# Two mixing attentions regrouped into turns of two units, and the router's last logits moved ahead of table and key products

## The chip, the cores and the metric

The kernel runs on one core of one Trainium2 chip. The metric is the device time in microseconds (us), lower being better; the median of three runs is compared. Engine names are those of the profile: PE (TensorE matmuls), PEld (its weight loads), DVE (VectorE), ACT (ScalarE), POOL (GpSimd), SP (SyncE, which issues most DMAs). All data are float32.

## What is computed

The reference is a two-block transformer on 512 tokens of width 1024; each block has two layers. The first block's layers end with a mixture of experts. For every token a router picks a group and two experts:

```python
g_logits = xt @ w_group
_, g_sel = lax.top_k(g_logits + b_group, 1)
e_logits = (xt @ w_expert).reshape(T, N_GROUPS, EXPERTS_PER_GROUP)[tok, g_sel]
_, e_local = lax.top_k(e_logits + e_bias, TOP_K)
```

The second block's two layers begin with a mixing attention each. Layer 0 is the dilated attention (16 heads of 64, three dilation patterns, which the kernel folds into one additive mask), layer 1 the differential attention (8 pairs of heads):

```python
p = softmax(q k^T / 8 + mask);           o = p v                       # dilated, per head
p = softmax over keys, for two maps;     o = (p[0] - lam * p[1]) v      # differential, per pair
o = rms_norm(o, sub_g) * (1 - lam_init)                                # differential only
```

Both are followed by the output projection `o @ w_out`, a cross attention to 256 memory tokens and a gated feed-forward layer.

## The kernel before

All five engines run one program each, in an order written out by hand; they meet on semaphores. `ps` is PSUM in eight banks of 512 columns, `TT` = 4 tiles of 128 tokens, `KC` = 8 chunks of 128 channels.

**Units.** An attention is cut into `UNITS` = 32 units: unit `n` is chunk `c = n // 4` (two heads, or one pair) and query tile `t = n % 4`. `PAIRED` = 16. For each chunk, q and k are first transposed (`turn_q`, `turn_k`, bank 7) and copied out (`queries` on ACT, `keys` on DVE).

**Dilated** (lines 2036 to 2186). PE: `scores(n)` (L2059), two products of 64 rows by 512 columns that lie in the two row halves of the array, into banks `2 * (n % 2)` and the next; it waits for `masked(n - 2)`. DVE: `masked(n)` (L2118) adds the mask, writes the tile and its row maximum. ACT: `expo(n)` (L2155), exponent and row sum. DVE: `invert(n)` (L2125). POOL: scales by the reciprocal (L2184). PE: `turn_probs(n)` (L2070), eight transposes into banks 4 and 5. ACT and DVE: `copy_probs(n)` (L2163, L2131). PE: `output(b, part)` (L2083), the product with v of two units at once into column halves of the array, in two parts of eight instructions. ACT: `finish(c)` (L2167) copies the finished chunk. The PE order is per unit `i`: `scores(i)`, `turn_probs(i - 2)`, a turn of q or k in two units of four, `output(i // 2 - 2, i % 2)`. The output projection starts after `finish(7)` (L2769).

**Differential** (lines 2213 to 2430). PE: `scores(n)` (L2247), as above, waiting for `expo(n - 2)`. DVE: `maximum(n)` (L2310). ACT: `expo(n)` (L2357). DVE: `invert(n)` (L2317). POOL: `weigh(n)`, which is a 128x1 product (L2400), a drain, and the scaling of the second map (L2402). DVE: `mixed(n)` (L2323), first map times reciprocal plus the weighed second map; both are in SBUF. PE: `turn_diff(n)` (L2256), four transposes. ACT: `copy_diff(n)` (L2365). PE: `output(n)` (L2265). DVE: `finish(n)` (L2329) copies the output, ACT: `square(n)` (L2374). Per chunk, POOL's `roots(c)` (L2408 on) and `scale_out(c)` (L2417) normalize, PE turns the result (`turn_out`, L2236) and ACT copies it (`copy_out`, L2379). In DVE's order, `invert(i - 1)` and `mixed(i - 2)` follow `maximum(i)`. In POOL's order `roots(c)` follows `weigh(4c + 11)` and `scale_out(c)` follows `weigh(4c + 12)`. Once the last scores are done, `out_products` of chunks 0 to 3 (L2742) are put between the remaining steps.

**Router** (`first_out`, lines 1102 to 1197; `router`, lines 1615 on). After the mixer's output projection, token tile 3 is transposed (`turn_raw`, L1233), its logits are computed (`route_tile`, L431), DVE chooses the experts (`choose`), PE counts the ranks (`count_before` L1452, `count_inside` L1459), DVE marks the slots (`place`), PE sums the marks into a table (`table_tile`, L1497), and POOL's first `gather_rows` (L1738) fetches rows by that table. The rows are transposed at L1748. Between these steps stand products for the memory keys (`key_products`, L1339; ACT reads them at L1348), which are needed in any case. POOL issues the store of `normed` (L1249), and every gather waits for it.

```python
key_products(name, key_q, 0, keys, range(2))
turn_raw(name, eng, y0, TT - 1)
share_tile(name, eng, j0, TT - 1, buf)
place_tile(name, eng, l, TT - 2)
key_products(name, key_q, 0, keys, range(2, 4))
table_begin(name, eng, l)
route_tile(name, eng, l, j0, TT - 1)
```

Of the kernel before, what the change touches and what calls it, by code (L numbers as in the profile page):

```python
# [8 lines left out]
TT = S // P  # L9
KC = D // P  # L10
# [69 lines left out]
def program(nc, a):  # L80
# [5 lines left out]
    with ctx:  # L86
# [1015 lines left out]
        def first_out(name, eng, l, m_norm):  # L1102
# [92 lines left out]
            key_products(name, key_q, 0, keys, range(2, 4))  # L1195
            table_begin(name, eng, l)
# [408 lines left out]
        def table_begin(name, eng, l):  # L1605

            if name == "pe":
                open_bank(eng, until=(table_ready, l + 1))
                at["table"] = count[("pe", "bank")] - 1
                for t in range(TT - 2):  # L1610
                    table_tile(eng, l, t, bank_of(at["table"]))
            else:
                at["table"] = take(name, "bank")

        def router(name, eng, l):

            w = first_keys_w(name)
            table_q = at["table"]
            if name == "pe":
                open_bank(eng, "dve")  # L1620
                count_q = count[("pe", "bank")] - 1
                count_before(eng, l, TT - 1, bank_of(count_q))
                table_tile(eng, l, TT - 2, bank_of(table_q))
            else:
                count_q = take(name, "bank")
            key_products(name, at["first_keys"], 0, w, range(4, KC))
            key_read(name, eng, l, 0, 0, at["first_keys"], counted=False)
            key_q = key_open(name, 0)
# [5 lines left out]
            key_products(name, key_q, 1, w, range(2))  # L1634
# [16 lines left out]
            key_products(name, key_q, 1, w, range(2, KC))  # L1651
# [384 lines left out]
        def dilated_pe(pe):  # L2036
# [36 lines left out]
            def output(b, part):  # L2073
                c, half = divmod(b, 2)
                if part == 0:
                    pe.wait_ge(l_probT_act, 2 * b + 2)
                    pe.wait_ge(l_probT_dve, 2 * b + 2)
                    if half == 0 and c:
                        pe.wait_ge(l_out_read, c)
                for s in range(2 * part, 2 * part + 2):  # L2080
# [4 lines left out]
                if part:  # L2085
                    m.then_inc(l_out, 1)
# [3 lines left out]
            for i in range(UNITS + 3):  # L2090
                if i < UNITS:
                    scores(i)
                if 0 <= i - 2 < UNITS:
                    turn_probs(i - 2)
                if i % TT == 1 and i // TT + 1 < KC:
                    turn_q(i // TT + 1)
                if i % TT == 2 and i // TT + 1 < KC:
                    turn_k(i // TT + 1)
                if i >= 4:
                    output(i // 2 - 2, i % 2)  # L2100
            output(PAIRED - 1, 1)

        def dilated_dve(dve):
# [30 lines left out]
            for i in range(UNITS + 2):  # L2134
                if i < UNITS:
                    masked(i)
                if 0 <= i - 1 < UNITS:
                    invert(i - 1)
                if i % TT == 2 and i // TT + 1 < KC:
                    keys(i // TT + 1)  # L2140
                if 0 <= i - 2 < UNITS:
                    copy_probs(i - 2)

        def dilated_act(act):
# [25 lines left out]
            for i in range(UNITS + 3):  # L2170
                if 0 <= i - 2 < UNITS:
                    copy_probs(i - 2)
                if i < UNITS:
                    expo(i)
                if i % TT == 1 and i // TT + 1 < KC:
                    queries(i // TT + 1)
                if i >= 6 and i % TT == 2:
                    finish(i // TT - 1)
# [34 lines left out]
        def differential_pe(pe, l):  # L2213
# [57 lines left out]
            for i in range(UNITS + 5):  # L2271
                if i < UNITS:
                    scores(i)
                if 0 <= i - 5 < UNITS:
                    output(i - 5)
# [1511 lines left out]
```

## Time and profile before

| what | value |
|---|---|
| median of 3 runs | 2943.52 us (2942.08 to 2946.53) |
| the profiled execution | 2939.72 us |
| its span, first to last instruction | 2937.9 us |
| PE busy | 2819.7 us, 96% of the span |
| DVE, ACT, POOL busy | 38%, 23%, 17% |
| mean granted PE clock | 0.993 of full speed |
| dilated attention | 1333.6 to 1450.1 us |
| differential attention, to the end of its first output products | 2214.9 to about 2346 us |
| the router, layer 0 and layer 1 | 306 to 324 us and 887 to 904 us |

All stage positions are microseconds from the start of the span. A timeline row gives start, duration, engine, line, operation, tiles, and how many instructions are merged in it; in brackets stands the engine's idle time before it and what ended that. One fp32 matmul of the source appears as two PE instructions. A windows row gives, for a stretch, the busy time and instructions of each engine, the granted PE clock and the DMA share.

### The profile page before, as it was taken

The numbers are of one execution on the slowest core, as the hardware profiler recorded it, in microseconds if no ns is written. First come the engines' busy times: TensorE is split into PE (matmuls) and PEld (weight loads), VectorE is DVE, ScalarE is ACT, GpSimd is POOL, SyncE is SP. The second block draws the span as 40 slices with busy tenths as digits, with TensorE's granted clock in tenths as the row PEclk, the third lists the DMA queues.
The fourth block names the chain that finished last, engine by engine and source line by source line (L and its number), as shares of the span: only waits on it lengthen the run. The fifth ranks groups of instructions, "written<-read, shape, count | busy, mean of one in ns | idle before, by whom it ended". The sixth has DMA issues, their size and how long they took to land.

```text
span 2937.9 us, 32164 instructions
## 1 busy us (share of the span) xinstructions
PE 2819.7 (96%) x12444; PEld 1898.3 (65%) x12444; DVE 1111.5 (38%) x2252; ACT 662.8 (23%) x1512; POOL 511.3 (17%) x785
## 2 busy tenths in 40 slices
PE   8999999799999987999999999999999999999998
PEld 4565543255655432685566688888686575788887
DVE  4543311154433111445432333354446432333354
ACT  3333110133331101105422211101206512211100
POOL 3101111131111111113200022201114410122201
PEclk9999999999999999999999999999999999999999
DMA  3206799821158998320021222222220121222222
GB/s 134 75 29 251 295 425 424 367 110 56 46 241 330 424 424 358 143 86 30 29 79 37 79 91 89 72 79 94 86 87 29 34 82 33 82 87 86 72 87 86
DMA packets 106579, 422.13 MB, mean 144 GB/s; under 512 B 10096, under 2 KB 14320, under 8 KB 91440
## 3 DMA queue, kind: packets, MB, share of 16 engines
q1 hardware_dynamic: 93104, 387.01, 33.9%
q0 software_dynamic: 12736, 30.84, 2.8%
q8 instruction: 104, 1.70, 0.2%
q10 hardware_dynamic: 576, 2.10, 0.2%
q14 instruction: 59, 0.48, 0.0%
HBM read 408.63 MB, written 27.26 MB: 148 GB/s over the span
## 4 chain that ended last, share of the span: by engine, by line
PE 77%; issue 9%; DMA 7%; DVE 2%; ACT 2%; POOL 1%; POOLq 1%; DVEq 0%; SPq 0%; ACTq 0%
PE ps L2536 35%; DMA ring_feat<-in_w 6%; PE ps L1773 6%; PE ps L2769 5%; PE ps L431 5%; PE ps L1112 3%; PE ps L2742 3%; PE ps L1814 3%; PE ps L2643 2%; PE ps L2789 2%; PE ps L3103 2%; PE ps L1339 2%; PE ps L2247 1%; PE ps L2265 1%; PE ps L2083 1%
## 5 line engine op out<-in xcount | busy, mean ns | idle before, releaser
L431 PE MATMUL ps<-ring_feat 128*128 128x512 f32 (+2 forms) x704 | 275.4, 546 | 4.9 <-DMA ring_feat<-in_w_lat 2.8
L2536 PE MATMUL ps<-ring_feat 128*128 128x256 f32 x1216 | 276.9, 379 | 0.8 <-ACT big L287 0.8
L2536 PE MATMUL ps<-big 128*128 128x256 f32 x1200 | 268.1, 379 | 0.0
L2536 PEld LDWEIGHTS ps<-ring_feat 128*128 128x128 f32 x1216 | 231.2, 190 | 33.1 <-issue 2.1
L2536 PEld LDWEIGHTS ps<-big 128*128 128x128 f32 x1200 | 228.3, 190 | 30.7
L431 PEld LDWEIGHTS ps<-ring_feat 128*128 128x128 f32 x704 | 133.0, 192 | 130.8 <-issue 93.8
L2769 PE MATMUL ps<-ring_feat 128*128 128x512 f32 x320 | 139.4, 593 | 0.7 <-ACT ring_feat L2167 0.7
L2536 PE MATMUL ps<-tmp 128*128 128x256 f32 x576 | 128.2, 379 | 0.0
L2536 PE MATMUL ps<-ring_feat,tmp 128*128 128x256 f32 x544 | 126.6, 379 | 0.0
L2536 PEld LDWEIGHTS ps<-tmp 128*128 128x128 f32 x576 | 109.6, 190 | 14.8
L1112 PE MATMUL ps<-ring_feat 128*128 128x512 f32 x256 | 114.7, 600 | 0.0
L2536 PEld LDWEIGHTS ps<-ring_feat,tmp 128*128 128x128 f32 x544 | 103.4, 190 | 14.0
L1789 DVE TENSOR_TENSOR tmp<-tmp,ps 128x256 f32<-128x256 f32 x32 | 13.5, 422 | 250.0 <-ACT tmp L1783 250.0
L2769 PEld LDWEIGHTS ps<-ring_feat 128*128 128x128 f32 x320 | 60.1, 190 | 73.3 <-issue 72.2
L1828 POOL DMA_INDIRECT expert_out<-tmp,route_i x32 | 32.1, 1004 | 405.1 <-ACT tmp L1823 393.6
L1773 PE MATMUL ps<-big,tmp 128*64 128x512 f32 x416 | 93.4, 596 | 6.2 <-DVE tmp L1757 4.7
L2536 PE MATMUL ps<-ring_feat,big 128*128 128x256 f32 x400 | 95.5, 379 | 0.0
L2725 DVE TENSOR_TENSOR big<-ps,par 128x512 f32<-128x512 f32 x32 | 22.1, 692 | 189.6 <-ACT big L2721 189.6
L1773 PE MATMUL ps<-ring_feat,tmp 128*64 128x512 f32 x384 | 86.2, 596 | 5.3 <-DMA ring_feat<-in_w 2.9
L1757 DVE TENSOR_TENSOR tmp<-ps,par 128x512 f32<-128x512 f32 x64 | 41.2, 686 | 131.1 <-PE ps L1748 131.1
L2742 PE MATMUL ps<-ring_feat 128*128 128x512 f32 x192 | 85.7, 596 | 5.0 <-ACT ring_feat L3002 2.7
L2536 PEld LDWEIGHTS ps<-ring_feat,big 128*128 128x128 f32 x400 | 76.1, 190 | 10.3
(497 smaller groups left out, 4630.8 us busy)
## 6 DMA issues: line engine op xcount, KB each, us to landing
big<-in_w SPq DMA_DIRECT2D x36, 2048.0 KB, 22.6
ring_feat<-in_w SPq DMA_DIRECT2D x36, 2048.0 KB, 29.2
ring_feat<-in_w_gate_up SPq DMA_DIRECT2D x22, 2048.0 KB, 8.0
ring_feat<-in_w_mix_in SPq DMA_DIRECT2D x12, 2048.0 KB, 8.2
e_spare<-in_w SPq DMA_DIRECT2D x12, 1792.0 KB, 25.7
par<-in_w SPq DMA_DIRECT2D x12, 1536.0 KB, 23.7
ring_feat<-in_w_down SPq DMA_DIRECT2D x12, 1536.0 KB, 6.7
tmp<-in_w_mem_kv SPq DMA_DIRECT2D x6, 2048.0 KB, 25.3
```

The lines of the kernel that those rows point to most:

```text
L431: yield T.matmul(bank, lhs(k), rhs(k), start=k == 0, stop=k == n - 1)
L1112: m = T.matmul(bank, featv[:, k, t * P:(t + 1) * P], w[:, k, :], start=k == 6, stop=k == 2)
L1339: m = T.matmul(bank_of(q)[:, 0:N_MEM], w[:, k, i * P:(i + 1) * P], memT[:, k, :], start=k == 0, stop=k == KC - 1)
L1757: m = V.tensor_tensor(e_xT[p % 2][:, 4 * b:4 * b + 4, :], ps[:, b, :].rearrange("p (k s) -> p k s", k=4), g[:, 4 * b:4 * b + 4].unsqueeze( ...
L1773: m = T.matmul(ps[h, u, :], e_xT[s][:, k, h], e_half(l, c, i)[k % 4], start=k == 0, stop=k == KC - 1)
L1814: m = T.matmul(ps[h, 6 + half, :], e_hT[:, k, h], e_half(l, c, i)[2 * k + half], start=k == 0, stop=k == 1)
L2536: m = T.matmul(to, lhs[:, j, :], rhs[:, j, :], start=start and j == 0, stop=stop and j == chunks - 1)
L2643: yield T.matmul(bank, featv[:, k, t * P:(t + 1) * P], w[:, k, :], start=k == 0, stop=k == KC - 1)
L2742: m = T.matmul(begun["banks"][t], featv[:, k, t * P:(t + 1) * P], begun["w"][:, k, :], start=k == 0, stop=k == KC - 1)
L2769: yield T.matmul(bank, featv[:, k, t * P:(t + 1) * P], w[:, k, :], start=k == 0, stop=k == KC - 1)
L2789: m = T.matmul(bank[:, tokens], w[:, k, (f % 4) * P:(f % 4 + 1) * P], featv[:, k, tokens], start=k == 0, stop=k == KC - 1)
L3103: m = T.matmul(bank[:, tokens], w[:, kk, o:o + P], featv[:, kk, tokens], start=kk == 0, stop=kk == KC - 1)
```

## The change

Nothing is computed differently; the orders are new. In both attentions PE issues the scores of two units back to back. In the dilated attention the two parts of `output` are joined, and at the end output-projection products stand between the last steps. In the differential attention DVE, ACT and POOL get new orders too. In the router, `route_tile` of the last tile comes before the table and before two key products, and the key products stand elsewhere in the chain.

```diff
 # first_out
             place_tile(name, eng, l, TT - 2)
-            key_products(name, key_q, 0, keys, range(2, 4))
-            table_begin(name, eng, l)
             route_tile(name, eng, l, j0, TT - 1)
 # router (table_begin is gone)
+                open_bank(eng, until=(table_ready, l + 1))
...
                 count_before(eng, l, TT - 1, bank_of(count_q))
-                table_tile(eng, l, TT - 2, bank_of(table_q))
+                for t in range(TT - 1):
+                    table_tile(eng, l, t, bank_of(table_q))
-            key_products(name, at["first_keys"], 0, w, range(4, KC))
+            key_products(name, first_q, 0, w, range(2, 4))
 # count_inside, place
-            key_products(name, key_q, 1, w, range(2))
+            key_products(name, first_q, 0, w, range(4, 6))
 # last table_tile, table_ready
-            key_products(name, key_q, 1, w, range(2, KC))
+            key_products(name, first_q, 0, w, range(6, KC))
+            key_read(name, eng, l, 0, 0, first_q, counted=False)
+            key_q = key_open(name, 0)
+            key_products(name, key_q, 1, w, range(KC))
 # dilated_pe
+            for p in range(PAIRED):
+                scores(2 * p)
+                scores(2 * p + 1)
+                if p >= 1:
+                    turn_probs(2 * p - 2)
+                if p % 2 == 0 and p // 2 + 1 < KC:
+                    turn_q(p // 2 + 1)
+                if p % 2 == 1 and p // 2 + 1 < KC:
+                    turn_k(p // 2 + 1)
+                if p >= 2:
+                    output(p - 2)
+                if p >= 1:
+                    turn_probs(2 * p - 1)
+            turn_probs(UNITS - 2)
+            output(PAIRED - 2)
+            turn_probs(UNITS - 1)
+            pe.wait_ge(l_masked, UNITS)
+            out_begin(pe)
+            pe.wait_ge(l_out_read, KC - 2)
+            out_products(pe, 0, range(KC - 2))
+            output(PAIRED - 1)
+            for t in range(1, TT):
+                if t == 1:
+                    pe.wait_ge(l_out_read, KC - 1)
+                out_products(pe, t, range(KC - 1))
 # dilated_dve, per p: masked(2p), masked(2p+1), copy_probs(2p-2), invert(2p), keys if p is odd, invert(2p+1), copy_probs(2p-1)
 # dilated_act, per p: expo(2p), copy_probs(2p-2), queries if p is even, expo(2p+1), finish(p//2-1) if p is odd, copy_probs(2p-1)
 # differential_pe
+            for p in range(PAIRED):
+                m, odd = divmod(p, 2)
+                scores(2 * p)
+                scores(2 * p + 1)
+                if not odd and m >= 4:
+                    turn_out(m - 4)
+                if p >= 2:
+                    output(2 * p - 4)
+                if p >= 1:
+                    turn_diff(2 * p - 2)
+                if odd and m + 1 < KC:
+                    turn_k(m + 1)
+                if p >= 2:
+                    output(2 * p - 3)
+                if not odd and m + 1 < KC:
+                    turn_q(m + 1)
+                if p >= 1:
+                    turn_diff(2 * p - 1)
...
 # differential_dve
+            for p in range(PAIRED):
+                maximum(2 * p)
+                if p >= 1:
+                    mixed(2 * p - 1)
+                maximum(2 * p + 1)
+                if p >= 2:
+                    finish(2 * p - 4)
+                invert(2 * p)
+                if p % 2 == 1 and p // 2 + 1 < KC:
+                    keys(p // 2 + 1)
+                if p >= 2:
+                    finish(2 * p - 3)
+                mixed(2 * p)
+                invert(2 * p + 1)
...
 # differential_act, per p: expo(2p), copy_out if even and late, copy_diff(2p-2), expo(2p+1), square(2p-4), queries if even, copy_diff(2p-1), square(2p-3)
 # differential_pool
-                if n >= 11 and n % TT == 3:
-                    roots((n - 11) // TT)
-                if n >= 12 and n % TT == 0:
-                    scale_out((n - 12) // TT)
+                if n >= 8 and n % TT == 0:
+                    roots((n - 8) // TT)
+                if n >= 9 and n % TT == 1:
+                    scale_out((n - 9) // TT)
```

## Rows read from the trace of the kernel before

**Rows 1.** Page, part 1: busy time of the engines over the span.

```profile
PE 2819.7 (96%) x12444; PEld 1898.3 (65%) x12444; DVE 1111.5 (38%) x2252; ACT 662.8 (23%) x1512; POOL 511.3 (17%) x785
```

**Rows 2.** Windows: dilated start and middle, differential middle (PE, PEld, DVE, ACT, POOL, PEclk, DMA).

```profile
1333.00:1347.00 14.00, 9.58 (x46) 5.03 (x47) 7.42 (x22) 7.29 (x16) 3.00 (x5) 0.88 0.43 150
1399.00:1412.00 13.00, 12.83 (x90) 7.17 (x86) 8.34 (x25) 8.38 (x23) 4.97 (x8) 1.00 0.00 0
2256.00:2270.00 14.00, 14.00 (x93) 9.38 (x91) 10.65 (x19) 12.23 (x38) 10.23 (x21) 1.00 0.01 2
```

**Rows 3.** Timeline of the dilated attention, PE: scores, transposes, output.

```profile
1381.50 1.13 PE L2059 MATMUL ps<-tmp 64*128 64x512 f32 x4
...
1385.03 1.13 PE L2059 MATMUL ps<-tmp 64*128 64x512 f32 x4
...
1386.09 1.09 PE L2070 MATMUL ps<-cst,tmp 128*128 128x128 f32 x8
...
1387.11 1.08 PE L2083 MATMUL ps<-tmp,big 128*64 128x256 f32 x8
...
1388.13 1.13 PE L2059 MATMUL ps<-tmp 64*128 64x512 f32 x4
...
1425.45 1.13 PE L2059 MATMUL ps<-tmp 64*128 64x512 f32 x4
```

**Rows 4.** Timeline of the dilated attention's end and the projection behind it, PE.

```profile
1442.45 1.06 PE L2070 MATMUL ps<-cst,tmp 128*128 128x128 f32 x8 [1.23 <-ACT tmp L2163]
...
1446.47 2.89 PE L2083 MATMUL ps<-tmp,big 128*64 128x256 f32 x24
...
1450.05 12.28 PE L2769 MATMUL ps<-ring_feat 128*128 128x512 f32 x28 [0.69 <-ACT ring_feat L2167]
```

**Rows 5.** Timeline of the differential attention, PE: scores, output, transposes; the fifth is twelve units on.

```profile
2239.34 1.13 PE L2247 MATMUL ps<-tmp 64*128 64x512 f32 x4
...
2240.40 1.16 PE L2265 MATMUL ps<-big,tmp 128*128 128x128 f32 x8
...
2241.39 0.60 PE L2256 MATMUL ps<-cst,tmp 128*128 128x128 f32 x4
...
2241.92 1.13 PE L2247 MATMUL ps<-tmp 64*128 64x512 f32 x4
...
2276.43 1.13 PE L2247 MATMUL ps<-tmp 64*128 64x512 f32 x4
```

**Rows 6.** Timeline of the differential attention, DVE and POOL.

```profile
2222.70 0.15 DVE L2317 RECIPROCAL stat<-stat 128x2 f32<-128x2 f32 x1
...
2223.36 0.69 POOL L2402 TENSOR_SCALAR tmp<-tmp,stat 128x512 f32<-128x512 f32 x1 [0.17 <-issue]
...
2226.18 0.73 DVE L2323 SCALAR_TENSOR_TENSOR tmp<-tmp,stat 128x512 f32<-128x512 f32 x1
...
2226.83 1.22 DVE L2310 TENSOR_REDUCE stat<-ps 128x2 f32<-128x1024 f32 x1
...
2242.26 0.96 POOL L2402 TENSOR_SCALAR tmp<-tmp,stat 128x512 f32<-128x512 f32 x1 [0.17 <-issue]
...
2265.72 0.24 POOL L2408 TENSOR_SCALAR stat<-stat 128x4 f32<-128x4 f32 x1
...
2267.82 0.33 POOL L2400 TENSOR_TENSOR stat<-stat 128x1 f32<-128x1 f32 x1
```

**Rows 7.** Timeline of the router, PE, layer 0; the last row is layer 1's.

```profile
309.24 1.98 PE L431 MATMUL ps<-par,ring_feat 128*128 128x36 f32 x16
...
312.29 3.52 PE L1339 MATMUL ps<-cst,ring_feat 128*128 128x256 f32 x8
...
323.34 1.09 PE L1748 MATMUL ps<-cst,tmp 128*128 128x128 f32 x8 [0.52 <-DMA tmp<-normed,route_i]
...
893.23 2.00 PE L1339 MATMUL ps<-cst,ring_feat 128*128 128x256 f32 x8
```

**Rows 8.** Window of one microsecond in layer 0's router (columns as in Rows 2).

```profile
312.00:313.00 1.00, 1.00 (x10) 0.87 (x9) 0.77 (x6) 0.00 (x0) 0.00 (x0) 0.50 0.88 352
```

More of the change, by code:

```diff
@@ L1603, in gate_weights, with router @@
                             gate.unsqueeze(1).to_broadcast([P, 2, TT]), ALU.mult)
-        def table_begin(name, eng, l):
+        def router(name, eng, l):
+            w = first_keys_w(name)
+            first_q = at["first_keys"]
             if name == "pe":
                 open_bank(eng, until=(table_ready, l + 1))
[L1609 to L1619, printed above, removed]
+                table_q = count[("pe", "bank")] - 1
                 open_bank(eng, "dve")
@@ L2071, in turn_probs, with output @@
                 m.then_inc(l_probs_turned, 1)
-            def output(b, part):
+            def output(b):
                 c, half = divmod(b, 2)
[L2075 to L2080, printed above, removed]
+                pe.wait_ge(l_probT_act, 2 * b + 2)
+                pe.wait_ge(l_probT_dve, 2 * b + 2)
+                if half == 0 and c:
+                    pe.wait_ge(l_out_read, c)
+                for s in range(TT):
                     for j in range(2):
@@ L2084, in output @@
                                      l_probT[b % 2][:, j, s, :], start=s == 0, stop=s == TT - 1)
-                if part:
-                    m.then_inc(l_out, 1)
+                m.then_inc(l_out, 1)
             turn_q(0)
             turn_k(0)
[L2090 to L2101, printed above, removed]
+            for p in range(PAIRED):
[23 more added lines that the diff above has]
+                out_products(pe, t, range(KC - 1))
         def dilated_dve(dve):
@@ L2133, in dilated_dve @@
             keys(0)
[L2134 to L2142, printed above, removed]
+            for p in range(PAIRED):
+                masked(2 * p)
+                masked(2 * p + 1)
+                if p >= 1:
+                    copy_probs(2 * p - 2)
+                invert(2 * p)
[3 more added lines that the diff above has]
+                if p >= 1:
+                    copy_probs(2 * p - 1)
+            copy_probs(UNITS - 2)
+            copy_probs(UNITS - 1)
         def dilated_act(act):
@@ L2169, in dilated_act @@
             queries(0)
[L2170 to L2178, printed above, removed]
+            for p in range(PAIRED):
+                expo(2 * p)
+                if p >= 1:
+                    copy_probs(2 * p - 2)
+                if p % 2 == 0 and p // 2 + 1 < KC:
+                    queries(p // 2 + 1)
+                expo(2 * p + 1)
+                if p >= 3 and p % 2 == 1:
+                    finish(p // 2 - 1)
+                if p >= 1:
+                    copy_probs(2 * p - 1)
+            copy_probs(UNITS - 2)
+            copy_probs(UNITS - 1)
+            finish(KC - 1)
         def dilated_pool(pool):
```

99 lines of the change are left out of this document (52 added, 47 removed).

## The prediction

> **What bounds the kernel now.** I first read the page's busy times: PE is busy in 96% of the span, no other engine in half of it [rows 1]. So a gain must take time out of PE's own sequence, and it can be lost only where another engine makes PE wait. The windows show the same inside both attentions: 12.83 of 13 us and 14.00 of 14 us of PE busy [rows 2]. But the reader should not stop there. In the differential stage DVE, ACT and POOL are busy for 10.65, 12.23 and 10.23 us of the 14 [rows 2]; all four engines are near their limit, and the order in which they hand work on counts. In the dilated stage DVE and ACT use 8.3 of 13 us and POOL 5.0, which leaves room.
>
> Then the timeline, since a busy PE need not be working at its pace. In the dilated stage scores start at 1385.03, transposes at 1386.09, the output part at 1387.11, the next scores at 1388.13: 1.06, 1.02 and 1.02 us, a unit of 3.10 us [rows 3]. What does each group need by itself? A pass of 512 columns takes 12.28/28 = 0.44 us in the projection, start of the next pass 0.43 [rows 4]; a unit's scores are two passes in each row half side by side, 0.86. In the undivided run of 24 output instructions, 16 more than usual took 2.89 - 1.08 = 1.81 us, 0.90 per eight with a short wait in it, so 0.86 as well [rows 3, 4]. I take 0.86 for all three groups. What is left, 0.20 behind scores and 0.16 behind each of the others, comes wherever the shape that PE uses changes (64 rows, full, 64 columns), and three times per unit. It is not the semaphore: the second part of an output has no wait of its own, and its gap is the same. These gaps are what the change goes after. The Trainium skill says so too (TensorEngine Tiling (Array Packing), Key Properties): changing the tiling mode drains the engine. It gives no price.
>
> **Dilated attention, steady part.** A unit with a turn of q or k takes 1385.03 - 1381.50 = 3.53, so a turn costs 0.43. A chunk of four units takes (1425.45 - 1385.03)/3 = 13.47 us [rows 3]. That is 4 x 3.10 + 2 x 0.43 = 13.26 and 0.21 of waiting behind ACT's `finish`. After the change a pair is two scores 1.72 + 0.20, transposes 0.86, a turn 0.43, a gap 0.16, output 1.72 + 0.16, transposes 0.86 + 0.16: 6.27 us, and a chunk 12.54. It saves 0.93. Can the others follow? 13 us of the stage hold 13/3.37 = 3.9 units, in which DVE is busy for 8.34, ACT for 8.38 and POOL for 4.97 us [rows 2]: 4.3, 4.3 and 2.6 us for two units, all under 6.27. In latency, the transposes of unit i stand two units and the next scores behind its own scores, 2 x 3.10 + 1.06 = 7.3 us where no turn lies between, and PE doesn't wait for POOL there today [rows 3]. In the new order they stand a pair and two scores behind, 6.27 + 1.92 = 8.2 us. So I see no new wait, and the 0.21 goes, since `finish` now stands behind the exponents. Seven and a half chunks: -7.0 us.
>
> **Dilated start and drain.** The start is a chain with nothing in flight, and PE's granted clock is 0.88 there [rows 2]. Two scores go first as before, but the second transposes now stand behind `turn_k` and wait for two copies: +0.6. The drain of before runs from the last scores, 1425.45 + 12.61 (three more plain units and the wait) = 1438.1, to the projection at 1450.05: 12.0 us for nine groups of 0.86, so 4.3 lost; one wait of 1.23 is in the rows [rows 4]. Afterwards six products of 0.86 cover the copy ahead of the last output, and seven per tile cover the last `finish`; what stays is a wait of about 1.3 for a copy ahead of `turn_probs(30)` and some gaps: -2.2. The projection does not get longer, since these are its own products done earlier. **Dilated: -8.6**, bounds -5 (half of the gaps stay) and -11 (no loss at the start, the wait of 1.3 gone).
>
> **Differential attention.** Here scores to output take 1.06, output to transposes 0.99, transposes to scores 0.53: 2.58 per unit; twelve units took 2276.43 - 2241.92 = 34.51 us, 11.50 per chunk with two to three turns [rows 5]. By PE alone a pair would need 1.92 + 0.99 + 0.43 + 0.89 + 0.53 = 4.76 and a chunk 9.52 + 1.1 = 10.6. But PE does not decide alone. DVE's new order puts `mixed(2p - 1)` ahead of `maximum(2p + 1)` and `invert(2p + 1)` behind `mixed(2p)`. `mixed` waits for POOL's `weigh`, and `weigh` waits for `invert`. So the two engines hand each unit to and fro with nothing overlapped: invert(2p), weigh, mixed(2p), invert(2p + 1), weigh, mixed(2p + 1), maximum(2p + 3), finish, invert(2p + 2). In the old order `mixed` came one turn later, and the loop reached over two units. The durations: reciprocal start to the end of `weigh` 2224.05 - 2222.70 = 1.35 when nothing disturbs POOL, mixed 0.65 to the next instruction, the reduction 1.15 (busy for 1.22, but the next begins before its end), `finish` about 0.2 (an estimate, for 128 columns where the reduction has 1024) [rows 6]. A pair takes 2 x 1.35 + 2 x 0.65 + 1.15 + 0.2 = 5.35; a chunk 10.7. `roots` (2.10 us from 2265.72 to 2267.82) now stands between two `weigh` calls, where only mixed and the next invert, 0.9, run beside it: +1.2. And it overlaps with `mixed`, both of whose inputs are in SBUF. L2402 takes 0.96 instead of 0.69 in such a place [rows 6], so I add 0.3: 12.2 us per chunk from the third chunk on, 0.7 more than now.
>
> The Trainium skill bears on this (SBUF - State Buffer, Who interferes with whom): a DVE instruction with two SBUF inputs keeps GpSimd's reads off the port they share. The two durations of L2402 agree. It helps here as well, since `weigh` no longer runs beside `mixed`.
>
> Sum: six chunks x 0.7 = +4.2; the second chunk, before any `roots`, -1.0; the start, where a longer chain must pass before the pairs flow, +1.0; the drain, whose steps are covered by output products before and after, -1.2. That is +3.0; I take **+2.5**, since some of `roots` may hide while a turn of q, k and output makes PE late. Bounds: -5 (PE alone: 11.50 - 10.6 = 0.9 on six chunks) and +10 (each `weigh` 0.27 longer, 1.1 per chunk more).
>
> **Router.** Both layers. The logits move ahead of four key instructions, 1.1 us at the pace of the eight that take 2.00 [rows 7], and of the first tables, but must then wait some 0.4 (an estimate) for the transposed tile's copy. In the chain from the logits to the table stood twelve key instructions, eight of them 3.52 us in layer 0 [rows 7]; now eight short ones stand there. I estimate that the table is ready 2.5 us sooner. Against it: every gather also waits for the store of `normed`, which is not moved, and PE waits only 0.52 us for the gathered rows today [rows 7]. The key products are done in any case. So at most 0.5 per layer, less the new short waits: -0.3. Against it stands the clock. In layer 0 the granted clock is at half, 1.2 GHz instead of 2.4 [rows 8], right after the logits, and eight key instructions take 3.52 us where layer 1 has 2.00 [rows 7]. In the new order transposes, logits, counts and tables follow each other with no key product between; a fall of the clock in layer 1 too costs about 1.5. No row shows the new order, so I take the two together as 0, bounds -1 and +4.
>
> **Sum.** -8.6 + 2.5 + 0 = -6.1 us. The profiled execution took 2939.72, 3.8 below the median of 2943.52; against its own time 2933.6, against the median 2937.4. No DMA is moved past another on POOL's or SP's queue; the load of the memory keys for the cross attention waits for the last output and so starts ahead of most of the projection, as it does now.
>
> **Rivals.** (A) *The differential loop does not bind*, because PE's turns are late enough to cover POOL. Then that stage gives -5, the whole -13.5: 2930. For it: DVE is idle for a part of each turn. Against it: the loop is a chain by program order, and it adds up to more than PE's 10.6. (B) *`weigh` stays at its contended length or the loop is longer still*: differential +10, the whole +1: 2945, no change. For it: most of the 32 calls took 0.96; against it, they ran beside `mixed`, and in the new order they cannot. (C) *The gaps do not belong to the change of shape* but to each group, so that pairs save nothing. Only drain and `finish` are left, -4, with the differential loop unchanged: -1.5, 2942. The undivided 24 instructions speak against it [rows 4]. (D) *PE falls to half clock in the differential stage.* New waits of about 1.5 us per chunk leave PE less busy. One stretch at half clock cost 3.52 - 2.00 = 1.5 us in the router [rows 7, 8]. In the steady part of both attentions the clock is at full today [rows 2]. If it fell in each of seven chunks for two such stretches, that is 7 x 3.0 = 21 us, the whole +15, 2958; it decides from 12 us on, which is eight stretches, where the sum passes +5.9.
>
> **How the numbers follow.** A measurement of this kernel can tell 0.2%, 5.9 us. Forecast (differential between 0 and +5, total -3 to -10): 0.62, half of it beyond 5.9. A: 0.17, all faster. B: 0.10, nearly all unchanged. C: 0.06, unchanged. D: 0.05, slower. Faster 0.31 + 0.17 and a little from the dilated bound, 0.50; slower 0.05 and a part of B, 0.07; the rest, 0.43, within. The range from 2930 to 2945 takes in the forecast, most of A and half of B.
>
> **What would show it.** Dilated: scores starts in pairs 0.86 apart, pairs 6.27 apart, a chunk 12.5 against 13.47; the projection's first products between the last output steps. If pairs are 6.7 apart, the gap theory is wrong. Differential: chunks of 12.2, PE waiting for L2304 or L2323, POOL's L2402 at 0.69, and DVE waiting for L2402. Chunks of 10.6 mean A, of 13 and more B. Router: L1641 some 2.5 us nearer to the logits, the gather where it was in layer 1, and the granted clock at half behind the logits in one or both layers. The forecast is wrong if any stage outside these three moves by over 2 us.

## The result, and the profile after it

The changed kernel took 2944.88 us, median of 12 runs (2942.93 to 2952.22); the kernel before, timed beside it, 2940.30 (2937.08 to 2946.53, 12 runs). The ratio is 1.0016, 95% interval 1.0009 to 1.0024: 4.7 us slower (2.6 to 7.1), where 6.1 us faster was forecast. The profiled execution has a span of 2941.9 us against 2937.9, also +4.0. The difference is within the bound of 5.9 us, so by that bound it is no change; but it is of the other sign, and it hides three parts that are each as large as itself or larger.

PE's busy time fell by 2.8 us [rows 1] and the span grew by 4.0, so PE waits longer. Page, part 1, of the changed kernel:

```profile
PE 2816.9 (96%) x12444; PEld 1904.2 (65%) x12444; DVE 1111.0 (38%) x2252; ACT 662.7 (23%) x1512; POOL 509.1 (17%) x785
```

The windows of the same stretches as in [rows 2], the first moved by the 6 us that the dilated stage now starts later (columns: length, PE, PEld, DVE, ACT, POOL, PEclk, DMA share, GB/s):

```profile
1339.00:1353.00 14.00, 10.20 (x40) 5.06 (x40) 7.36 (x24) 7.10 (x16) 3.37 (x5) 0.76 0.42 150
1399.00:1412.00 13.00, 13.00 (x92) 7.99 (x90) 8.83 (x27) 8.92 (x22) 5.87 (x10) 1.00 0.01 1
2256.00:2270.00 14.00, 12.20 (x73) 8.07 (x72) 9.20 (x17) 9.88 (x31) 8.60 (x17) 0.88 0.01 2
```

The middle of the dilated stage is better filled than before. In the differential stage PE is busy for 12.20 us of 14 instead of 14.00, every engine does less, and the granted clock averages 0.88.

**Where the time went.** I compared the starts of the same work in both timelines. The transposes of the first gathered rows are at 326.21 instead of 323.34 [rows 7], 2.9 us late; in layer 1 they are 6.7 us late. The dilated stage starts 6.3 late, and the memory queries behind its output projection start 1.8 early: the stage gave 8.1. Up to the differential stage 1.0 of it is lost again (PE waits 0.78 us for a copy ahead of the second part of these queries), and the differential stage then costs 4.8. 6.3 - 8.1 + 1.0 + 4.8 = 4.0, the difference of the spans.

*Dilated*, PE's timeline, one pair and its ends, against [rows 3, 4]:

```profile
1404.51 1.99 PE L2051 MATMUL ps<-tmp 64*128 64x512 f32 x8
1406.43 1.09 PE L2062 MATMUL ps<-cst,tmp 128*128 128x128 f32 x8
1407.35 0.60 PE L2034 MATMUL ps<-cst,big 128*128 128x128 f32 x4
1407.88 1.95 PE L2074 MATMUL ps<-tmp,big 128*64 128x256 f32 x16
1409.76 1.09 PE L2062 MATMUL ps<-cst,tmp 128*128 128x128 f32 x8
1410.79 1.99 PE L2051 MATMUL ps<-tmp 64*128 64x512 f32 x8
...
1446.26 5.32 PE L2784 MATMUL ps<-ring_feat 128*128 128x512 f32 x12
1451.51 1.95 PE L2074 MATMUL ps<-tmp,big 128*64 128x256 f32 x16
```

A pair takes 1410.79 - 1404.51 = 6.28 us (forecast 6.27), with no wait in it, and twelve products stand ahead of the last output.

*Differential*, the vector engine and POOL around one pair with `roots`, against [rows 6]:

```profile
2256.82 0.75 DVE L2347 SCALAR_TENSOR_TENSOR tmp<-tmp,stat 128x512 f32<-128x512 f32 x1 [0.98 <-POOL tmp L2445]
...
2257.56 1.20 DVE L2334 TENSOR_REDUCE stat<-ps 128x2 f32<-128x1024 f32 x1
2260.62 0.75 DVE L2347 SCALAR_TENSOR_TENSOR tmp<-tmp,stat 128x512 f32<-128x512 f32 x1 [1.85 <-POOL tmp L2445]
2261.29 1.22 DVE L2334 TENSOR_REDUCE stat<-ps 128x2 f32<-128x1024 f32 x1
...
2256.87 0.80 POOL L2451 TENSOR_SCALAR stat<-stat 128x4 f32<-128x4 f32 x1
...
2258.51 1.04 POOL L313 TENSOR_TENSOR stat<-stat 128x4 f32<-128x4 f32 x1
2259.52 0.19 POOL L2443 TENSOR_TENSOR stat<-stat 128x1 f32<-128x1 f32 x1
2259.89 0.69 POOL L2445 TENSOR_SCALAR tmp<-tmp,stat 128x512 f32<-128x512 f32 x1 [0.17 <-issue]
2260.78 2.20 POOL L2460 TENSOR_SCALAR big<-big,stat 128x128 f32<-128x128 f32 x4 [0.19 <-issue]
```

The four instructions of `roots` (L2451 to L313) keep POOL from 2256.87 to 2259.52, 2.65 us. The second weighing of the pair (L2443, L2445) stands behind them, the mixing (L2347) waits 1.85 us for it, and the next maximum (L2334) stands behind the mixing. L2451 takes 0.80 beside a mixing, where the same instruction took 0.24 [rows 6]. `scale_out` (L2460) follows behind the second weighing. PE's first scores of a chunk and their wait for the key copy, which is queued behind all this:

```profile
2250.89 1.99 PE L2259 MATMUL ps<-tmp 64*128 64x512 f32 x8 [1.33 <-DVE tmp L2328]
...
2263.41 3.39 PE L2259 MATMUL ps<-tmp 64*128 64x512 f32 x8 [1.33 <-DVE tmp L2328]
```

From the third on chunks take 12.47, 12.53, 13.26, 12.52 and 12.24 us (11.5 before, the mean of three [rows 5]). After one of the waits the scores take 3.39 instead of 1.99: half clock, once behind the start of the stage, in the chunk of 13.26.

*Router*, layer 0, against [rows 7]; first SyncE's and POOL's queues in the kernel before (the last line is the store's time to its landing):

```profile
311.24 0.33 SPq L1707 DMA_DIRECT2D ring_feat<-in_w  x1
...
309.75 0.62 POOL L1249 DMA_DIRECT2D normed<-tmp  x1 [1.47 <-ACT tmp L333]
319.02 1.12 POOL L1738 DMA_INDIRECT tmp<-normed,route_i  x1 [8.65 <-DVEq L1644]
...
normed<-tmp POOLq DMA_DIRECT2D x1, 512.0 KB, 5.5
```

and in the changed kernel:

```profile
310.02 0.33 SPq L1699 DMA_DIRECT2D ring_feat<-in_w  x1
...
309.73 0.62 POOL L1247 DMA_DIRECT2D normed<-tmp  x1 [1.47 <-ACT tmp L333]
321.82 1.12 POOL L1730 DMA_INDIRECT tmp<-normed,route_i  x1 [11.48 <-DMA normed<-tmp]
...
normed<-tmp POOLq DMA_DIRECT2D x1, 512.0 KB, 11.2
```

Then PE in the changed kernel:

```profile
311.43 2.07 PE L1337 MATMUL ps<-cst,ring_feat 128*128 128x256 f32 x4
...
326.21 1.09 PE L1740 MATMUL ps<-cst,tmp 128*128 128x128 f32 x8 [1.77 <-DMA tmp<-normed,route_i]
```

What the two queues moved in 312 to 314 us, the kernel before first and then the changed one, and in 314 to 320 us of the changed one (q1 is SyncE's queue, q0 is POOL's):

```profile
q0 software_dynamic: 131, 0.48, 60.2%
q1 hardware_dynamic: 30, 0.31, 38.1%
...
q1 hardware_dynamic: 39, 0.44, 69.9%
q0 software_dynamic: 42, 0.17, 21.7%
...
q1 hardware_dynamic: 112, 1.64, 68.8%
q0 software_dynamic: 96, 0.34, 13.9%
```

Two things are new. SyncE's 2 MB load of slot FEAT waits for the last logits and so is issued 1.2 us sooner, 0.3 us behind the start of the store of `normed` instead of 1.5. The store lands 11.2 us after its issue, in layer 1 11.3, where it took 5.5 and 7.3 before. In the kernel before, 131 packets of its queue run within 2 us, against 30 of SyncE's. In the changed kernel POOL's queue has 144 packets and 0.52 MB, the store's, spread from 311 to 321 us. They run beside those of the load, also 144 (288 and 4.19 MB for two loads), about one for one. The gather, which waited for the table in layer 0 before (DVEq), now waits for the store. The second new thing is the clock, which is at half in both layers for some 7 us (four key products take 2.07 instead of 1.1):

```profile
312.00:318.00 6.00, 6.00 (x24) 4.58 (x23) 1.91 (x10) 0.00 (x0) 0.00 (x0) 0.50 0.93 345
896.00:902.00 6.00, 6.00 (x23) 4.59 (x23) 1.90 (x10) 0.00 (x0) 0.00 (x0) 0.51 0.97 374
```

### The profile page after: what moved, and what is told of

The parts are those of the page before. It is cut to its first block, busy times and chain, and to the rows that moved or that the text cites. A ratio compares the mean times of both kernels' runs of the same rounds, so it can differ in the third digit from the quotient of the medians.

```text
span 2941.9 us, 32161 instructions
## 1 busy us (share of the span) xinstructions
PE 2816.9 (96%) x12444; PEld 1904.2 (65%) x12444; DVE 1111.0 (38%) x2252; ACT 662.7 (23%) x1512; POOL 509.1 (17%) x785
## 4 chain that ended last, share of the span: by engine, by line
PE 72%; issue 11%; DMA 8%; POOL 3%; DVE 2%; ACT 2%; POOLq 1%; DVEq 0%; SPq 0%; ACTq 0%
PE ps L2578 35%; DMA ring_feat<-in_w 6%; PE ps L1765 6%; PE ps L431 4%; PE ps L2784 4%; PE ps L2811 4%; PE ps L1806 3%; PE ps L1112 2%; PE ps L2685 2%; PE ps L2831 2%; PE ps L3145 2%; PE ps L1337 1%; PE ps L2062 1%; PE ps L2074 1%; PE ps L2051 1%
## 5 line engine op out<-in xcount | busy, mean ns | idle before, releaser
L2578 PEld LDWEIGHTS ps<-ring_feat 128*128 128x128 f32 x1216 | 230.9, 190 | 34.5 <-issue 3.3
L431 PEld LDWEIGHTS ps<-ring_feat 128*128 128x128 f32 x704 | 132.7, 191 | 131.0 <-issue 93.6
L2784 PEld LDWEIGHTS ps<-ring_feat 128*128 128x128 f32 x256 | 47.6, 190 | 64.4 <-issue 57.5
L2811 PEld LDWEIGHTS ps<-ring_feat 128*128 128x128 f32 x256 | 48.0, 190 | 57.4 <-issue 57.4
```

The source lines that it names most:

```text
L431: yield T.matmul(bank, lhs(k), rhs(k), start=k == 0, stop=k == n - 1)
L2578: m = T.matmul(to, lhs[:, j, :], rhs[:, j, :], start=start and j == 0, stop=stop and j == chunks - 1)
L2784: m = T.matmul(begun["banks"][t], featv[:, k, t * P:(t + 1) * P], begun["w"][:, k, :], start=k == 0, stop=k == KC - 1)
L2811: yield T.matmul(bank, featv[:, k, t * P:(t + 1) * P], w[:, k, :], start=k == 0, stop=k == KC - 1)
```

## The experiments

Each ratio is to the kernel before, timed on the same chip; the groups of runs were on four chips, so runs of two groups are compared by their ratios. The profiled executions differ by up to 4.3 us ahead of any edit (first key products of layer 0 at 304.2 to 308.5), so inside the router I read a distance: from the first key products of the last tile (305.09 before) to the transposes of the first gathered rows (323.34), 18.25 us in layer 0 and 16.60 in layer 1.

**Each part alone.** First the router's part.

> Only the router's part of the change; both attentions stay as before. Theory (late gather): the changed kernel's gather starts 2.8 us later in layer 0 and 6.9 in layer 1 than before, the second less the first being 4.0 of its own, and nothing behind the router gives it back before the dilated stage. So the whole is +6 to +7 us against the kernel before, and the first pass of the dilated scores starts 6.3 us later. Rival (the router is worth 0, as predicted, and the shift seen behind it comes from something in the changed attentions, such as another placing of the code): within 1 us of the kernel before.

Ratio 1.0021 (1.0012 to 1.0030): +6.2 us. Distances 20.48 and 19.85 us; POOL waits 10.9 and 11.1 us behind the store for it to land. The loss is the router's own.

The dilated part:

> Only the dilated part. Theory (the pairs save the gaps between shapes, as in the changed kernel's trace): chunks of 12.5 us, the stage 8.1 us shorter, of which 0.8 to 1.0 is lost again at the start of the memory queries behind it; the whole -7 to -8 against the kernel before. Rival (the gaps do not belong to the shapes): chunks of 13.4, the whole -2 to -3.

Ratio 0.9973 (0.9963 to 0.9982): -7.9 us. Four pairs take 1381.76 - 1356.65 = 25.11 us, a chunk 12.56. The gaps do belong to the changes of shape:

```profile
1369.20 1.99 PE L2059 MATMUL ps<-tmp 64*128 64x512 f32 x8
1371.12 1.09 PE L2070 MATMUL ps<-cst,tmp 128*128 128x128 f32 x8
...
1375.48 1.99 PE L2059 MATMUL ps<-tmp 64*128 64x512 f32 x8
```

The differential part:

> Only the differential part. Theory (the loop DVE, PE, ACT, DVE, POOL, DVE binds, longer than predicted): chunks of 12.2 to 12.6 us against 11.2 to 11.65, the stage +4.8, the whole +4.8 against the kernel before, between +4 and +6. Rival (the stage was long because its start was shifted by what stands ahead of it, so that the roots met other work): +2.5 or less.

Ratio 1.0019 (1.0009 to 1.0028): +5.6 us, chunks of 12.5 to 13.3 from the third on, the half clock in the same chunk (scores of 3.58 us). The three parts sum to 6.2 - 7.9 + 5.6 = +3.9; the whole change gave +4.7 (2.6 to 7.1).

**The router's load.** With the store first, that is, with SyncE's load waiting until the store has landed:

```
                 sp.wait_ge(bank_full, feat_free[l])
+                sp.wait_ge(normed_rest, 16 * (TT - 1) * (l + 1))
                 load_chunk(sp, l, FEAT)
```

> The router's part alone, and SyncE issues the 2 MB weight load of slot FEAT only once the store of the normed rows has landed. Theory DMA order (the store, issued in the same microsecond as before, lands 11.2 us after its issue instead of 5.5 because the 2 MB load was issued ahead of it): the store lands after some 5 us again in both layers, the gather starts about 1 to 2.5 us sooner than in the kernel before, as the table is ready sooner, and the whole is -2 to +3 us against the kernel before; what is left above that is the half clock, about 1.5 us for each stretch. Rival (clock alone): the gather is late because the products behind the logits run at half clock and delay the table; then this wait brings nothing, the gather of layer 1 starts over 5 us later than before and the whole stays at +6.

Ratio 1.0020 (1.0011 to 1.0029): +5.9, outside what my theory expected and the rival's total. But the gather of layer 1 starts only 0.3 us later than before, counted from the first key products, not over 5, so it is not the rival's mechanism either. The order did what it should to the store: it lands after 5.7 us in layer 0 and 6.0 in layer 1, and the gather of layer 0 starts 1.7 us nearer to the first key products than before. But the distances are 19.37 and 19.23. In layer 0 the load, now at 315.13, is in flight when the gather is issued, and the rows come 7.1 us behind the gather, before 4.3:

```profile
317.02 1.12 POOL L1730 DMA_INDIRECT tmp<-normed,route_i  x1 [7.00 <-DVEq L1633]
...
324.11 1.09 PE L1740 MATMUL ps<-cst,tmp 128*128 128x128 f32 x8 [1.56 <-DMA tmp<-normed,route_i]
```

So in layer 0 I had only moved the collision from the store to the gather. In layer 1 PE does not wait for the rows at all: it is late itself, at half clock. To take the load away from both:

```
+                for s in range(2):
+                    sp.wait_ge(rows_in[s], 16 * (PAIRS // 2 * l + 1))
                 load_chunk(sp, l, FEAT)
```

> The changed router alone, and SyncE issues the 2 MB load of slot FEAT behind the landing of the first two gathers (its first reader comes 30 us later). Theory (the 2 MB load, wherever it starts, delays the small transfer issued just behind it: the store in the change, the gather in the two runs with the store first): the store lands after 5 to 6 us, the gather after 4, and what is left is PE's own time at half clock: 19 us from the first key products to the transposed rows at most in both layers, with no wait for the gathered rows over 0.5; the whole +1.5 to +4 against the kernel before. Rival (the clock costs nothing where the gather is waited for, so that the transfers are all of the router's loss): 17 to 18 us in both layers, the whole -1 to +1.

Ratio 0.9998 (0.9989 to 1.0007). Distances 16.59 and 19.17: the same code twice in one execution, once at full clock and once at half (the two ends of each distance, then a window of 7 us in each layer, PEclk behind the POOL column):

```profile
305.31 1.03 PE L1337 MATMUL ps<-cst,ring_feat 128*128 128x256 f32 x4
...
321.90 1.03 PE L1740 MATMUL ps<-cst,tmp 128*128 128x128 f32 x8
...
886.65 1.03 PE L1337 MATMUL ps<-cst,ring_feat 128*128 128x256 f32 x4
...
905.82 1.03 PE L1740 MATMUL ps<-cst,tmp 128*128 128x128 f32 x8
...
311.00:318.00 7.00, 6.73 (x58) 5.40 (x57) 4.71 (x26) 0.38 (x1) 1.18 (x2) 1.00 0.36 145
892.00:899.00 7.00, 7.00 (x49) 5.58 (x49) 3.10 (x19) 0.29 (x1) 0.00 (x0) 0.56 0.44 178
```

In neither layer do the rows make PE wait. Seven microseconds at half clock cost 2.6 us once the transfers are out of the way. The total is below what was expected, +1.5 to +4, and inside the rival's -1 to +1; in the profiled execution that is because layer 0 had full clock, and how the other executions ran is not known.

**The key products.** With the store first, key products 2 and 3 again ahead of the last logits:

> As the run with the store first, but key products 2 and 3 (four instructions of 256 columns, 1.11 us) stand ahead of the last logits again, as before the change; the rest of the new router order stays. Theory clock (the run of narrow instructions from the last transposes over logits, counts and tables to the next key products is what PE's clock falls after): that run is broken by 1.1 us of wide products, the half clock goes from 7 us in each layer back to 3.4 us or none, and the stretch from the first key products to the first transposes of the gathered rows takes 17 to 18 us in both layers instead of 19.4 and 19.2; the whole is 2 to 4 us below the run with the store first, -2 to +1 against the kernel before. Rival (those stretches are long because the products that are now behind the logits have nothing to hide the gather's own latency): still over 19 us in both layers, the whole as with the store first.

Ratio 1.0011 (1.0002 to 1.0020): +3.2 us. Distances 19.51 and 20.48: not what the clock theory said. The half clock did shrink (0.98 in 312 to 314, 0.50 only in 314 to 316 and 0.67 in the next two), but PE waited 1.30 us for one-hot rows and 0.85 and 1.75 for the gathered rows, which came 7.7 and 8.0 us behind the gather. So less half clock gave no shorter distance, and the rows are what PE waits for. Then the wide products placed between all the narrow ones, and the load behind the gathers:

```
 route_tile:   key_products(..., range(2, 4)) ahead of it
 router:       tables, key_products(..., range(4, 6)), count_inside,
               range(6, 7), table_tile, range(7, KC)
```

> As the run before, and key products 2 and 3 stand ahead of the last logits, 4 and 5 between the tables and the count behind them, 6 and 7 behind the count and the last table: every run of narrow instructions is cut by wide ones, and PE does not wait there for the one-hot rows (1.30 us in the run with the keys ahead). Theory (clock and transfers are both needed, and each alone makes the rows late): no half clock or 3.4 us of it, 16.5 to 17.5 us from the first key products to the transposed rows in both layers, the whole -2 to 0 against the kernel before. Rival (the clock falls whatever stands between): over 18.5 us, the whole +1.5 or more.

Ratio 0.9996 (0.9987 to 1.0005), full clock in both layers (1.00 over the same windows), 16.58 and 16.57 us, as expected. That the wide products keep the clock up is not shown by it: the last run below has this order and the half clock. The missing case is the late store at full clock: the change's own load, with key products 2 and 3 between logits and count:

> The changed router alone, the 2 MB load of slot FEAT where the change has it (behind the last logits), but the key products cut PE's narrow instructions: 2 and 3 behind the last logits and ahead of the count, 4 and 5 between the tables and the next count, 6 and 7 singly. Theory (the late store alone makes the gather late): at full clock the store still lands 10 to 11 us after its issue, the first gather starts over 10 us behind it, and the transposed rows come 19.5 to 20.5 us after the first key products in both layers, so that the half clock of the changed kernel was covered by this wait; the whole +3.5 to +5.5 against the kernel before. Rival (the causes add): 18 to 18.8 us, the whole +1 to +2.5.

Ratio 1.0026 (1.0015 to 1.0038): +7.6 us. Clock 1.00 in both windows, and still

```profile
312.27 0.33 SPq L1700 DMA_DIRECT2D ring_feat<-in_w  x1
...
311.97 0.62 POOL L1247 DMA_DIRECT2D normed<-tmp  x1 [1.47 <-ACT tmp L333]
323.21 1.12 POOL L1731 DMA_INDIRECT tmp<-normed,route_i  x1 [10.62 <-DMA normed<-tmp]
...
327.63 1.97 PE L1741 MATMUL ps<-cst,tmp 128*128 128x128 f32 x8 [3.64 <-DMA tmp<-normed,route_i]
```

Distances 20.32 and 20.75. The late store alone makes the router's loss; in the change it covers the half clock, which costs only when the store is in time. The total is above the forecast of either theory. After the waits for the rows, 3.64 and 4.08 us, PE is at half clock in both layers (transposes 1.97 instead of 1.09), which is one place more per layer; I did not separate it.

| load of FEAT | clock | runs (layer) | distance, us |
|---|---|---|---|
| 0.3 behind the store's issue | half | changed (0, 1); router alone (0, 1) | 21.14, 20.35; 20.48, 19.85 |
| 0.3 behind the store's issue | full | keys between (0, 1) | 20.32, 20.75 |
| behind the gathers | half | load behind gathers (1); all mended with router (0), the last run below | 19.17; 18.77 |
| behind the gathers | full | load behind gathers (0); with keys moved (0, 1) | 16.59; 16.58, 16.57 |

**The differential loop.** All three start from the differential part alone, +5.6 us. Chunks are given from the third on. One instruction per weighing:

```
-G.tensor_tensor(out=d_rinv[..., 1:2], in0=neg_lam, in1=d_rinv[..., 1:2], op=ALU.mult)
-pool.drain()
-G.tensor_scalar(d_prob[..., 1, :], d_prob[..., 1, :], d_rinv[..., 1:2], 1.0, ...)
+G.tensor_scalar(d_prob[..., 1, :], d_prob[..., 1, :], d_rinv[..., 1:2], neg_lam, ...)
```

> The differential part alone, with GpSimd's weighing of a unit in one instruction: the negative lambda is the second scalar of the multiplication of 512 columns, where 1.0 stood, and the tiny product ahead of it (0.19 us and 0.17 of drain) goes; the result is the same up to rounding. Theory (the turn waits for POOL): the vector engine's waits for POOL, 17.5 us over the stage, fall by 4 or more, a chunk is some 0.6 to 0.9 us shorter than the 12.5 to 13.3 now, the whole +0 to +2 against the kernel before instead of +5. Rival (PE's wait for the copied keys comes from the order on the vector engine alone): less than 1 us gained.

Ratio 1.0001 (0.9992 to 1.0010), +0.3; chunks of 11.7 to 12.0. `roots` and `scale_out` behind other units:

```
-if n >= 8 and n % TT == 0: roots((n - 8) // TT)
-if n >= 9 and n % TT == 1: scale_out((n - 9) // TT)
+if n >= 9 and n % TT == 1: roots((n - 9) // TT)
+if n >= 11 and n % TT == 3: scale_out((n - 11) // TT)
```

> The differential part alone, with GpSimd's roots behind the weighing of units 9, 13, ... and its scaling behind 11, 15, ..., where both stood between the two units of every second pair (behind 8 and 9). Nothing is taken out. Theory (the roots, 0.80 + 0.23 + 0.25 + 1.04 and gaps, 2.7 us between two weighings of one pair, hold up the second, behind which the next maximum is queued): the 1.85 us wait for POOL in every chunk goes, with it PE's wait of 1.33 for the keys; a chunk takes 11.4 to 11.8, the whole -1 to +1.5 against the kernel before instead of +5. Rival (the loop of the two weighings alone binds, at the 5.35 per pair that was predicted, with chunks of 12.2): the place of the roots is worth 1 us at most, since POOL does the same work in a chunk.

Ratio 0.9988 (0.9979 to 0.9997), -3.5: nine microseconds for the place of two calls, more than I expected. Chunks of 10.6, 11.2, 11.4, 11.0, 11.0, and no half clock in them. PE's line of scores over 2210 to 2310 (idle before it behind the bar), in the changed kernel and then in this run:

```profile
L2259 PE MATMUL ps<-tmp 64*128 64x512 f32 x128 | 35.8, 680 | 6.8 <-DVE tmp L2328 6.7
```

```profile
L2247 PE MATMUL ps<-tmp 64*128 64x512 f32 x128 | 34.1, 651 | 1.5 <-DVE tmp L2316 0.8 <-ACT tmp L2376 0.3
```

The vector engine still waits 14.3 us for POOL in this window (17.2 in the changed kernel); but no single wait is over 1.2 us, and hardly any reaches PE.

The mixing one maximum later on the vector engine:

> The differential part alone, PE's pairs, ACT and POOL as in the change; on the vector engine the mixing of a unit stands one maximum later (maximum of 2p, reciprocal 2p-1, mixed 2p-2, maximum 2p+1, finish, reciprocal 2p, mixed 2p-1, keys, finish), so that a late weighing does not stand ahead of the maximum of the same pair. Theory (the chain by program order from a weighing over mixed to the maximum binds): a chunk takes 11.5 to 11.9, the vector engine waits for POOL less than 8 us over the stage, the whole 0 to +2 against the kernel before. Rival (PE's turns in pairs bind whatever the vector engine's order): chunks stay at 12.5 or more.

Ratio 0.9997 (0.9988 to 1.0006), -0.9, chunks of 11.6 to 11.7. The vector engine no longer waits for POOL:

```profile
L2335 DVE SCALAR_TENSOR_TENSOR tmp<-tmp,stat 128x512 f32<-128x512 f32 x30 | 22.2, 741 | 0.0
```

It was 17.2 us in the changed kernel. Each of the three edits to the loop alone takes away the loss.

**Mended versions.**

> Router as before; both attentions as in the change, the differential with the weighing in one instruction and with roots and scaling behind units 9 and 11 of every four. If the parts add up: dilated -8.0, differential -3.5 by the run with the spread roots, and 1 to 3 more for 0.36 us less in each weighing: -12 to -15 against the kernel before, chunks of 10.6 to 11.2 in the differential stage. If the two mends of the differential take away the same wait: -11 to -12.

Ratio 0.9963 (0.9950 to 0.9977), -10.9 us; chunks of 10.4 to 10.9 in the differential stage. The middle is nearest to -11 to -12, the case in which the two mends take away the same wait; the interval (-14.7 to -6.8) does not exclude the sum.

> As the run with both attentions mended, router as before, but the 2 MB load of slot FEAT behind the first two gathers. The kernel before issues that load 0.8 to 1.1 us behind the store, which lands after 5.5 and 7.3 us. Theory (the load touches the store even there): the gathers of both layers start up to 0.5 us sooner, and the whole is 0 to 2 us below the run with the attentions alone. Rival (a load issued behind the store does it no harm): equal within 1 us.

Ratio 0.9959 (0.9945 to 0.9972), -12.1; not to be told from the run before it. The gather of layer 0 starts 8.7 us behind the end of the store's issue (8.6 without the edit), that of layer 1 7.2 (7.4). So a load 1.5 us behind the store does the gather little harm. The store of layer 1 does land sooner, after 6.0 us for 7.2, but then the gather waits for the table.

> Both attentions mended as before, and the router with the 2 MB load behind the gathers and the key products moved (as in the run that had 16.6 us in both layers). If the parts add: 1 to 2 us below the run with all but the router's order, -13 to -14 against the kernel before. Rival (the stages behind take the gain back): as that run, -12.

Ratio 0.9950 (0.9936 to 0.9964), -14.7 us (-18.8 to -10.6): the fastest point measured, and faster than both kernels, but its interval overlaps the two others. In its profiled execution the half clock is back in the router (distances 18.77 and 17.26), although the order is the one that had full clock in both layers.

## Why the prediction was wrong

**The step that failed: the router, taken as 0** with bounds -1 and +4. It measured +6.2 alone and 6.3 in the trace of the whole. The prediction said that the store of `normed` "is not moved" and that "No DMA is moved past another on POOL's or SP's queue". Both are true and miss it: the load on SyncE's queue moves against the store on POOL's. The program text hides it: `feat_free` is taken behind `route_tile`, some 2,500 lines ahead of SyncE's wait for it. I costed the store at its old landing time, and the moved step released a 2 MB load 1.2 us sooner. By the table's row at full clock the late store is worth 20.3 - 18.3 = 2.1 us in layer 0 and 20.8 - 16.6 = 4.2 in layer 1 against the execution before. And a table that is ready sooner buys nothing there, since the gather waits for table and store both. The table was worth less than taken, too: where the gather waits for it and the clock is full, it starts 11.2 us behind the first key products in the new order (load behind gathers, layer 0) and 12.5 in the old (differential alone, layer 0), 1.3 us sooner and not 2.5.

**The clock** was named, with a fall in layer 1 at 1.5 us. It fell in both layers, for some 7 us and not for the 3.4 that layer 0 had before (0.76 over 7 us). That cost 2.2 to 2.6 us where it shows (18.77 and 19.17 against 16.57 and 16.59 in the table), and nothing measurable in the change, where the store is later still. What makes the clock fall stays open: it differs between executions of one order.

**Differential: right in mechanism, +4.8 in the trace and +5.6 alone against +2.5.** The loop over `weigh`, `mixed` and the maximum binds once `roots` stands in it, as written. Mis-sized is the term of `roots`, +1.2 and 0.3 for contention per chunk: the 2.10 us [rows 6] became 2.65 because its first instruction now runs beside a mixing, and I let 0.9 of it hide. What I left out is `scale_out`, 2.20 us, which follows at once behind the very next weighing; so a chunk's 4.9 us of POOL's other work fall into one pair. Chunks came to 12.2 to 12.5, and once, with the half clock, to 13.3, not to 12.2. The early chunks, 10.98 and 10.63 before any `roots`, went as forecast, but they do not show the loop: in the run with both mends PE's order gives 10.4 to 10.9. `weigh` at 0.69 was right too, so rival B's price was not paid; that B's total, 2945, is the measured one is chance, since B left the router at 0. Rival D, the half clock after new waits, came true once instead of fourteen times.

**Dilated: right,** -8.1 in the trace and -7.9 for the whole run alone, for -8.6. Pair 6.28 for 6.27. Some 0.8 to 1.0 us went again in a wait for a copy ahead of the memory queries. Rivals A and C fell.

The test that I had set, "wrong if any stage outside these three moves by over 2 us", did not fire. The fault was inside a named stage: the router's range, -1 to +4, was too narrow because its costs were looked for on PE and not on the DMA queues.

## What to carry to other kernels

When a step moves, list every counter that it raises and every engine that waits on one, SyncE's weight loads among them; a load released a microsecond sooner can cost more than it gives, if a small store or gather is issued beside it and sits on the path. Compare the packets of two such transfers, not only their bytes. Give a load that is not read for long a later wait: this one is issued at 310.02 and not read before 358.95. In a loop over several engines the place of a burst on one queue, here two calls between two weighings, can be worth more than its length, so spread it over the turns before shortening anything.

## What was unexpected of the hardware

- A 512 KB store takes 5.5 and 7.3 us when a 2 MB load is issued 1.5 us behind it, 5.5 to 5.6 and 6.0 to 6.6 when none is until the gathers have landed, and 11.2 and 11.3 when the load is 0.3 us behind the start of its issue, and so still ahead of its end (0.62 us). It then lands within a microsecond of the load (310.02 + 11.8). The load before it, issued 4.5 us ahead of the store, has nearly run out by then in both kernels. The Trainium skill says (DMA: Bandwidth & Descriptors, Queues, rings and completion order) that each DMA engine takes turns between its queues packet by packet. With the packets that the profile counts, the router's rows agree: store and load have 144 each, so in turns the store ends when the load does, though it has a quarter of the bytes. No run varies the packets to test it, and whether the skill's packets are those of the profile is not shown. In the kernel before, most of the store's packets ran before the load's began. The packets of the delayed gathers are not counted here.
- The granted clock in the router differs between executions of one code. Of seven profiled executions with the old router, five show 0.76 over 311 to 318 us (distance 18.2 to 18.5) and two 1.00 (17.5 and 17.7); in layer 1 two of seven show 0.76 or 0.78 (17.6), the others 1.00 (16.5 to 17.3). Layer 0 of the run with the load behind the gathers stayed at full clock where layer 1 did not. The Trainium skill (TensorE: Matmul & The Clock Gate, Part 1: The HAM clock gate) says that the number of slow matmuls at the start of one kernel varies between its runs. These rows show such a variation in the middle of a kernel. One profile does not settle such a term.
- POOL's first instruction of `roots`, on 128x4, takes 0.80 us beside a mixing on the vector engine and 0.24 without one.
